# Half steps of the chunk inverse on four array quadrants in a streaming-encoder kernel

## What is computed

```python
def step(S, inp):
    r_t, w_t, k_t, v_t, kk_t, a_t = inp
    sa = jnp.einsum('bhij,bhj->bhi', S, -kk_t)
    S = S * w_t[..., None, :] + sa[..., :, None] * (kk_t * a_t)[..., None, :] + v_t[..., :, None] * k_t[..., None, :]
    return S, jnp.einsum('bhij,bhj->bhi', S, r_t)
```

## Time and profile before

| what | value |
| --- | --- |
| median of 3 runs | 1891.11 us (1883.77 to 1899.21) |
| profiled execution, first to last instruction (span) | 1882.3 us |
| PE busy in the span | 1739.7 us, 92% |
| PEld, DVE, ACT, POOL busy | 1487.6, 1131.4, 682.7, 496.8 us |
| prompt mixing, tiles 1 to 8 | about 345 to 915 us of the span |

### The profile page before, as it was taken

One profiled execution on the slowest core, in us unless ns is written; L12 is line 12 of the kernel. 1 busy time (PEld: TensorE's weight loads), 2 busy tenths in 40 slices (PEclk: granted clock), 3 DMA queues, 4 the chain that ended last, 5 costly groups with the idle time before them and its releaser, 6 DMA issues. The chain is left out here.

```text
span 1882.3 us, 41252 instructions
## 1 busy us (share of the span) xinstructions
PE 1739.7 (92%) x17079; PEld 1487.6 (79%) x17079; DVE 1131.4 (60%) x1885; ACT 682.7 (36%) x1483; POOL 496.8 (26%) x399
## 2 busy tenths in 40 slices
PE   6999997888999999898799997999999989999997
PEld 5899995566666666666678876999999978888886
DVE  6611034557666656656434589656666555889797
ACT  2222112344444544544332225222322234453443
POOL 0000002322232132121200012555555431436302
PEclk9999997899999999999899998999999999999999
DMA  5553230111111110111406331444444477667642
GB/s 195 193 192 98 75 98 24 53 37 52 65 49 41 38 49 17 61 51 38 128 26 233 95 131 45 130 129 134 135 139 139 138 246 273 209 214 250 224 130 100
DMA packets 158031, 219.96 MB, mean 117 GB/s; under 512 B 34470, under 2 KB 96574, under 8 KB 156824
## 3 DMA queue, kind: packets, MB, share of 16 engines
q1 hardware_dynamic: 156524, 212.62, 34.6%
q0 software_dynamic: 1328, 4.78, 0.6%
HBM read 152.75 MB, written 65.43 MB: 116 GB/s over the span
## 5 line engine op out<-in xcount | busy, mean ns | idle before, releaser
L1657 PE MATMUL c_p<-c_d_b_hi,c_d_a_hi 128*128 128x512 f32 x448 | 175.8, 392 | 8.2 <-DVE c_d_b_lo L1430 6.5
L1657 PE MATMUL c_p<-c_d_b_hi,c_d_a_lo 128*128 128x512 f32 x448 | 175.3, 391 | 0.0
L1657 PE MATMUL c_p<-c_d_b_lo,c_d_a_hi 128*128 128x512 f32 x448 | 175.3, 391 | 0.0
L1617 PE MATMUL c_p<-c_T_hi,c_up_op_hi 128*128 128x288 f32 x512 | 113.0, 300 | 12.0 <-DVE c_T_lo L1327 8.4
L1186 ACT ACTIVATE c_d_a_hi<-c_a_raw 128x512 fp32r<-128x512 f32 x112 | 70.3, 627 | 125.6 <-PE c_p L1657 106.5
L1617 PE MATMUL c_p<-c_T_lo,c_up_op_hi 128*128 128x288 f32 x512 | 112.6, 299 | 0.0
L1617 PE MATMUL c_p<-c_T_hi,c_up_op_lo 128*128 128x288 f32 x512 | 112.5, 299 | 0.0
L323 ACT ACTIVATE a_o<-a_pO 128x308 f32<-128x308 f32 (+1 forms) x80 | 32.7, 408 | 219.8 <-PE a_pO L462 202.8
L1424 DVE TENSOR_TENSOR c_d_a_lo<-c_a_raw,c_d_a_hi 128x512 fp32r<-128x512 f32 x112 | 89.0, 794 | 38.4 <-ACT c_d_a_hi L1186 38.0
L1657 PEld LDWEIGHTS c_p<-c_d_b_hi,c_d_a_hi 128*128 128x128 f32 x448 | 84.6, 189 | 27.8 <-issue 10.3
L462 PE MATMUL a_pO<-a_wh,a_hT_hi 128*128 128x308 f32 x576 | 96.0, 309 | 9.4 <-DVE a_hT_lo L390 9.0
(11 more groups left out here) (512 smaller groups left out, 4475.4 us busy)
## 6 DMA issues: line engine op xcount, KB each, us to landing
c_a_raw<-scratch_ops SPq DMA_DIRECT2D x112, 256.0 KB, 3.4
c_d_r<-w_down SPq DMA_DIRECT2D x96, 256.0 KB, 4.2
c_up_raw<-w_up SPq DMA_DIRECT2D x32, 512.0 KB, 5.3
scratch_ops<-c_hid SPq DMA_DIRECT2D x64, 256.0 KB, 2.5
scratch_ops<-c_h_sum SPq DMA_DIRECT2D x48, 256.0 KB, 2.0
scratch_p<-a_o SPq DMA_DIRECT2D x72, 154.0 KB, 1.8
m_pr<-w_in SPq DMA_DIRECT2D x8, 1232.0 KB, 8.0
m_pr<-scratch_p SPq DMA_DIRECT2D x8, 1232.0 KB, 5.4
```

Source lines behind the costliest of these rows:

```text
L1617: last = pe.matmul(pS[U.slot[j, m]][:, h, 0:PIECE], w[:, k, :], x[:, k, PIECE * h:PIECE * h + PIECE], start=m in (1, 2, 5) and k == 0 and ...
L1657: last = pe.matmul(bank, d_a[G.a_slot(a)][x][:, P * p:P * p + P], d_b[b % DB_RING][w][:, :], start=m in (1, 2, 5) and j == 0 and n == 0, s ...
```

## The change

For the tiles of 128 tokens the squaring goes by half steps: the even heads (g = 0) and the odd heads (g = 1) are jobs of their own with a bank each of which they use 256 columns, and g = 1 runs one half step behind g = 0. `staggered` issues two jobs in turn, matmul by matmul: T(v,0) with X(v-1,1), and X(v,0) with T(v,1). An X job writes its chunk to the other half of the partitions (`crossed`), so one job of a pair uses the two quadrants on the diagonal and the other the two beside it. After an odd number of levels X lies exchanged; so T of an odd level needs A exchanged too. ACT makes this copy, `IAs`, kept in `OT`, in its part of `newton_t` of level 0, behind the exponential of head 1 and ahead of its copies of the weights of head 1. X(4,1) is a new step `newton_last` of its own, behind level 4. In the scan X and `zr` are read from the exchanged half. DVE makes F in two instructions of 256 columns a level, ACT copies X in two of 256 columns. The meta tile is unchanged.

```diff
@@ schedule
             steps += attend("score", v + 2) + outputs[v] + late
+        steps += [("newton_last", i, levels)]
         v = levels + 1
@@ phase_mix_prompt
+        IAs = heads(OT[:, :, :].rearrange("p k n -> p (k n)"))
...
+        def crossed(n, c, times):
+
+            return rows_of(n, c ^ times % 2 if n == P else c)
...
+            def staggered(i, *jobs):
+
+                banks = [J.fill(pe, (i, *job)) for job in jobs]
+                for k in range(PAIRS):
+                    for ck in range(2):
+                        for at, (name, v, g) in enumerate(jobs):
+                            h, x = 2 * k + g, XA if v else X0
+                            C = crossed(P, ck, v)
+                            lhs, rhs = (x, IAs if v % 2 else IA) if name == "T" else (F, x)
+                            to = C if name == "T" else crossed(P, ck, v + 1)
+                            ends[at] = pe.matmul(banks[at][to, CHUNK * k:CHUNK * k + CHUNK], lhs[C, h, :], rhs[C, h, :],
+                                                 start=True, stop=True)
+                for at in range(len(jobs)):
+                    J.filled(ends[at])
@@ tensor
-                if step == "newton_t":
+                if step == "newton_t" and n < P:
...
+                elif step == "newton_t":
+                    if v:
+                        J.wait_taken(pe, (i, "X", v - 1, 0))
+                        J.wait_taken(pe, (i, "T", v - 1, 1))
+                        if v == 1:
+                            pe.wait_ge(S("IA_crossed"), 2 * i)
+                        staggered(i, ("T", v, 0), ("X", v - 1, 1))
+                    else:
+                        J.wait_taken(pe, (i, "A", 0))
+                        J.wait_taken(pe, (i, "XC", 0))
+                        staggered(i, ("T", 0, 0))
-                if step == "newton_x":
+                if step == "newton_x" and n < P:
...
+                elif step == "newton_x":
+                    J.wait_taken(pe, (i, "T", v, 0))
+                    if v:
+                        J.wait_taken(pe, (i, "X", v - 1, 1))
+                    else:
+                        pe.wait_ge(S("A1_taken"), i + 1)
+                        J.wait_taken(pe, (i, "XC", 1))
+                    staggered(i, ("X", v, 0), ("T", v, 1))
+                if step == "newton_last":
+                    J.wait_taken(pe, (i, "T", v - 1, 1))
+                    staggered(i, ("X", v - 1, 1))
...
-                    if v == 0:
+                    if v == 0 and n < P:
                         J.wait_taken(pe, (i, "X", LEVELS[n] - 1))
...
+                    if v == 0 and n == P:
+                        for g in range(2):
+                            J.wait_taken(pe, (i, "X", LEVELS[n] - 1, g))
                     pe.wait_ge(S("zr_ready"), m + 1)
+                    Q = crossed(n, v, LEVELS[n])
@@ scalar
+                if s == "newton_t" and v == 0 and n == P:
+                    J.wait_taken(act, (i, "A", 0))
+                    act.wait_ge(S("A1_taken"), i + 1)
+                    if i >= 2:
+                        J.wait_filled(act, (i - 1, "OT"))
+                    for ck in range(2):
+                        act.activation(IAs[crossed(P, ck, 1), :, :], IA[rows_of(P, ck), :, :], ACT.Copy).then_inc(S("IA_crossed"), 1)
+                        act.wait_ge(S("IA_crossed"), 2 * (i - 1) + ck + 1)
+                if n == P and (s == "newton_x" or (s == "newton_t" and v) or s == "newton_last"):
+                    name, g = ((i, "X", v, 0), 0) if s == "newton_x" else ((i, "X", v - 1, 1), 1)
+                    bank = J.take(act, name)
+                    J.taken(act.activation(XA[:, g:HEADS:2, :], heads(bank[:, 0:PAIRS * CHUNK]), ACT.Copy), name)
@@ vector
+                if s in ("newton_t", "newton_x") and n == P:
+                    g = 0 if s == "newton_t" else 1
+                    bank = J.take(dve, (i, "T", v, g))
+                    J.taken(dve.scalar_tensor_tensor(F[:, g:HEADS:2, :], heads(bank[:, 0:PAIRS * CHUNK]), -1.0,
+                                                     twice_c.unsqueeze(1).to_broadcast([P, PAIRS, CHUNK]),
+                                                     ALU.mult, ALU.add), (i, "T", v, g))
```

More of the change, by code:

```diff
@@ L2241, in _ @@
                                   start=h < 2, stop=False, skip_group_check=True)
+                    if v == 0 and n == P:
+                        for g in range(2):
+                            J.wait_taken(pe, (i, "X", LEVELS[n] - 1, g))
                     pe.wait_ge(S("zr_ready"), m + 1)
+                    Q = crossed(n, v, LEVELS[n])
                     for h in range(HEADS):
-                        last = pe.matmul(bank_sa[out_rows(n, v, h % 2), HD * h:HD * h + HD], XA[R, h, 0:min(n, CHUNK)],
-                                         zr[R, HD * h:HD * h + HD], start=True, stop=True)
+                        last = pe.matmul(bank_sa[out_rows(n, v, h % 2), HD * h:HD * h + HD], XA[Q, h, 0:min(n, CHUNK)],
+                                         zr[Q, HD * h:HD * h + HD], start=True, stop=True)
                     J.filled(last)
@@ L2581, in _ @@
                     act.wait_ge(S("BTp_out"), i + 1)
-                if s == "newton_x":
+                if s == "newton_x" and n < P:
                     bank, m = J.take(act, (i, "X", v)), min(n, CHUNK)
                     J.taken(act.activation(XA[0:n, :, 0:m], heads(bank[0:n, :])[:, :, 0:m], ACT.Copy), (i, "X", v))
+                if s == "newton_t" and v == 0 and n == P:
[10 more added lines that the diff above has]
+                    J.taken(act.activation(XA[:, g:HEADS:2, :], heads(bank[:, 0:PAIRS * CHUNK]), ACT.Copy), name)
                 if s == "scan_z":
                     m = chunk_no(i, v)
-                    R = rows_of(n, v)
+                    Q = crossed(n, v, LEVELS[n])
                     act.wait_ge(S("z_ready"), m + 1)
@@ L2592, in _ @@
                     for g in range(2):
-                        last = act.activation(by_pair(zr[R, :])[:, g], Z[out_rows(n, v, g), g], ACT.Copy, scale=-1.0)
+                        last = act.activation(by_pair(zr[Q, :])[:, g], Z[out_rows(n, v, g), g], ACT.Copy, scale=-1.0)
                     last.then_inc(S("zr_ready"), 1)
@@ L2766, in _ @@
                                 J.taken(last, (i, name, g))
-                if s == "newton_t":
+                if s == "newton_t" and n < P:
                     bank = J.take(dve, (i, "T", v))
```

## The result

The changed kernel takes 1922.17 us (median of 4 runs, 1918.18 to 1928.58) against 1890.18 us for the kernel before (median of 4, 1883.77 to 1899.21): ratio 1.0169, 95% interval 1.0138 to 1.0201. It is slower by over 1%, and lies above the range of 1880 to 1913.

What follows compares the result with a forecast made beforehand. TensorE was taken as the fullest engine, with waits for other engines using up what shorter steps save. Waits and copies net +5.2 us, one clock drop +2: span 1889.5, forecast 1898 us against 1891.1 (+0.4%), range 1880 to 1913.

Steps and rivals of the forecast that it cites:

- The rate of four quadrants: Inverse steps on TensorE: 32 records on four quadrants take 0.56 us instead of 1.01, saving 0.45 a full step.
- Rival 3: Inverse steps: pairs don't overlap fourfold, a full step stays near 1.0 us; 1916 us, chance 0.05.
- rival 4: All eight tiles: the whole 32 us saved on TensorE is kept; 1859 us, chance 0.05.
- rival 1: Tiles 1 to 4 keep gains where banks allow, 11 us, tiles 5 to 8 even; 1880 us, chance 0.20.
- That the saving turns into waits: All tiles: 4.0 us a tile saved on TensorE goes into waits for ACT, DVE and banks; net +5.2 us.
- +5.2 net: Sum over all tiles before the clock: +5.6 us in tiles 5 to 8, -0.4 in tile 4.
- tiles 1 to 3: 0: Tiles 1 to 3: gains and losses cancel, 0 us each.
- tile 4 -0.4: Tile 4, one bank of weights and no wait for ACT in newton_x: sum -0.4 us, counted from level 2.
- the reset: Tile 4, level 2: the latents wait for DVE's norm, so the gain of earlier levels ends there.
- The wait in level 2 of tile 7: Level 2, tiles 5 to 7: the wait ahead of the weights' transposes grows from 1.71 to about 3.0 us.
- I count one: +2.: Level 2 waits of tiles 5 to 7: one new drop of TensorE's clock, costing 2 us.
- Rival 2: Waits ahead of transposes, levels 1 and 2: eight new clock drops, one a tile, +21 us; 1912 us, chance 0.12.

Runs made afterwards that it cites:

- f3: Changed kernel with ACT's copies of X(v-1,1) in levels 1, 3 and 4 put ahead of the exponential: 1913.68 us, ratio 1.0127.
- f4: Changed kernel with ACT's X copies of levels 1 to 4 ahead of the exponential and the next tile's latents behind level 2's newton_t on TensorE: 1905.79 us, ratio 1.0117.
- g2: f4 with the two jobs of a pair issued one after another instead of in turn: 1906.08 us, ratio 1.0094.
- f2: Kernel before with the next tile's latents moved behind newton_t of level 2 on TensorE alone: 1889.45 us, ratio 0.9996.
- e3: Changed kernel with the two jobs of a pair issued one after another instead of in turn: 1932.51 us, ratio 1.0230.
- f1: Changed kernel with idle matmuls in TensorE's waits, their number fitted to each tile and wait: 1912.18 us, ratio 1.0108.
- e2: Kernel before with idle 128x128 matmuls in TensorE's waits, 34 a tile: 1928.26 us, ratio 1.0225.
- g1: f4 with idle matmuls fitted to TensorE's waits: 1902.10 us, ratio 1.0067.
- g4: Kernel before with idle matmuls fitted to its waits: 1891.55 us, ratio 1.0011.

## Why the prediction was wrong

*The rate of four quadrants.* Right: 32 loads in 0.56 us. Rival 3 falls. PE saved 24.6 us on the inverse in tiles 2 to 8, but no tile from the second on got shorter; rival 4 (all kept) and rival 1 (some kept) fall too.

*That the saving turns into waits.* Right in sum. The forecast had 7 x 4.0 = 28 us of saving in these tiles and +5.2 net, so 33 us of new waits and added work; PE's idle time grew by 29.6. Its places were partly off. Right: `newton_x` of tiles 5 to 8 waits for the weights' copy, 15.7 us in 20 waits over all tiles. Mis-sized: in level 0 `newton_x` came 1.3 us late in tile 7 instead of 1.0, since the copies of A took 1.29. Missed: in level 1 of tiles 2 to 4 TensorE waits 0.75 to 0.97 us for X(0,1), whose copy stands behind the exponential and, on ACT, behind the square; I had put X(0,1) ahead of the square. Missed too: in level 2 it is `newton_t` that takes the bank of `cT`, so the wait moved from behind this step to ahead of it (14.2 us in 7 waits), where its gain can't shorten it. Missed as well: TensorE waits for DVE's F, 6.5 us in the group of `b_OT` above, up to 2.23 us at a time, where I had F only as a delay of a row maximum. So "tiles 1 to 3: 0" and "tile 4 -0.4" were wrong (the terms that I gave for tile 4 from the reset on, +0.85, -0.45, -0.7 and +0.3, add up to 0 besides): tiles 2 to 4 lost 3.9, 3.8 and 1.9 us, clock and all, and tiles 5 to 8 lost 4.5, 3.1, 6.3 and 6.6 where I had 1.4 each. f3 and f4, which work on the first two of these orders, gave 8.5 and 16.4 us by the medians. The wait in level 2 of tile 7 that should have neared 3 us isn't there: 0.92 ahead of `newton_t`, none ahead of the transposes.

*The clock, the step that failed.* "I count one: +2." The lost clock of tiles 2 to 8 grew from 10.2 to 41.0 us, 18 drops of 1.7 us more and not one, and the unchanged records took 26.7 us more. The price of a drop was about right; the count was wrong. The mistake has two parts. I counted a drop only where a single wait is longer than the one that had kept the clock (1.71 us in tile 7 of before), and so saw a risk in level 2 alone. The length of a wait doesn't decide it, and the trace of before could have told me: its level 2 waits of 1.73, 1.97, 2.21 and 1.80 us (tiles 2, 3, 4 and 6) were followed by a drop, those of 1.87 and 1.71 (tiles 5 and 7) were not, nor was one of 1.73 us in level 1 of tile 8. The change puts waits close together, 1.02 and 1.34 us with 0.98 us of work between them in level 0 of tile 7, 1.94 and 0.91 in level 1, and the clock fell behind both pairs; but it held behind 1.26 and 1.24 us in tile 8, so that isn't a rule either. And I had the saving itself only as time: f4 has 16.1 us less busy time than g2 with nearly the same idle time, and 11.0 us more in other matmuls, at the lower clock.

*The rivals.* Rival 2 named the mechanism, but with one drop of 2 us a tile (1912, chance 0.12). Tile 7 has two, of 1.7 and 3.4 us, and the kernel came to 1922. The rule cited with it (the Trainium skill, TensorE: Matmul & The Clock Gate, section HAM oscillation) fits the rows of tile 7, though not each wait here (tile 8). I let one row against it, the 1.71 us of tile 7, weigh more than tile 4's row for it.

*What stays open.* How the 26.7 us divide between the new waits and the shorter steps: no run has the waits of before with the half steps, or the new waits at a full clock without idle matmuls that cost time themselves. Why the clock fell behind some waits and held behind others of the same length is open too. The 7 us ahead of tile 1 are hardly the change's: in the profiled executions tile 2 starts anywhere from 417.1 to 426.0 us, and at 424.3 in f2, which has no half steps.

## What to carry to other kernels

In a kernel where TensorE is nearly full but waits every few microseconds, a cheaper TensorE step is worth only what passes both tests: is there no wait behind it, and does the clock hold with less work between the waits. Compare the busy time of instructions that the change does not touch: if the same records take longer than before and the granted clock is lower by the same share (here 7% and 6%), the loss is the clock's, and the list of waits won't show it. Before putting copies on a helper engine, list what stands ahead of them in its order; here two such places, the copy of A and X(0,1), became waits of TensorE.

## What the runs showed of the hardware

The two jobs of a pair overlap at their seam even when issued one after another. The weight loads of a pair in g2, first and last group:

```profile
784.04 0.46 PEld L2119 LDWEIGHTS b_R<-b_XC,b_F 64*64 64x64 f32 x12 [1.55 <-ACT m_ring L2695]
...
784.48 0.43 PEld L2119 LDWEIGHTS b_R<-b_IA,b_XC 64*64 64x64 f32 x11
```

From 784.04 to 784.91 they are 0.87 us, not the 1.01 of a step on two quadrants, so the order within the pair is worth 0.31 us a pair, 9 x 0.31 x 8 = 22 us in all and not the 32 of e3's queue theory. Half steps on four quadrants instead of two lowered the mean clock with the idle time all but unchanged (0.96 to 0.93, g2 to f4). The clock's drops in tiles 2 to 8 cost 1.7 us each or a multiple of it. Idle matmuls raise the clock (0.92 to 0.95 in f1), but at some 0.23 us each (the weight loads of 20 records take 2.31 us in e2) they win little: 10.0 us in f1, 3.7 in g1, nothing in g4.
